# All eight channel blocks of a depthwise convolution on TensorE, in 128x32 column tiles over shifted copies made through DRAM

## The reference

```python
def conformer_conv(x, w_pw1, b_pw1, dw_w, dw_b, ln_g, ln_b, w_pw2, b_pw2):
    a = x @ w_pw1 + b_pw1
    u = a[..., :D_MODEL] * jax.nn.sigmoid(a[..., D_MODEL:])
    u = lax.conv_general_dilated(u, dw_w[:, None, :].astype(u.dtype), window_strides=(1,),
        padding=[(CONV_WIDTH - 1, 0)], dimension_numbers=("NWC", "WIO", "NWC"),
        feature_group_count=D_MODEL) + dw_b
    u = jax.nn.silu(layer_norm(u, ln_g, ln_b))
    return u @ w_pw2 + b_pw2
```

## Time and profile before

| | |
|---|---|
| Time before, median of 3 runs | 1090.81 us (1090.73 to 1091.69) |
| The profiled execution's own time | 1090.82 us |
| Its span in the profile | 1088.8 us |
| PE busy, of the span | 1061.1 us (97%) |
| DVE busy | 706.8 us (65%) |
| ACT busy | 540.7 us (50%) |
| POOL busy | 22.6 us (2%) |

### The profile page before, as it was taken

The page is one execution under the profiler, slowest core; times in us unless marked ns, Lnnn a source line. Parts: engine busy times, 40 slices in busy tenths (PEclk is TensorE's granted clock), DMA queues, the critical chain, the costliest instruction groups (busy, mean ns, idle before and its releaser), DMA issues.

```text
span 1088.8 us, 13626 instructions
## 1 busy us (share of the span) xinstructions
PE 1061.1 (97%) x5484; PEld 899.6 (83%) x5484; DVE 706.8 (65%) x996; ACT 540.7 (50%) x698; POOL 22.6 (2%) x34
## 2 busy tenths in 40 slices
PE   8999899999999999999999999999999999999997
PEld 7998778888887778778888887878888888999886
DVE  5999875544548787776454545767554475777654
ACT  5853654444445666755444434565444553434533
POOL 1000310000000000000000000000000000000000
PEclk9999999999999999999999999999999999999999
DMA  8631365555553453256554555366545455455530
GB/s 322 193 100 39 106 223 197 190 193 193 193 175 144 151 188 117 78 199 246 193 193 174 179 191 191 122 216 232 191 177 194 157 191 193 157 192 193 194 116 39
DMA packets 27829, 188.68 MB, mean 173 GB/s; under 512 B 3016, under 2 KB 4168, under 8 KB 5880
## 3 DMA queue, kind: packets, MB, share of 16 engines
q1 hardware_dynamic: 24912, 179.32, 45.8%
q0 software_dynamic: 1392, 6.21, 1.7%
q10 hardware_dynamic: 1464, 2.30, 1.2%
HBM read 185.19 MB, written 2.62 MB: 173 GB/s over the span
## 4 chain that ended last, share of the span: by engine, by line
PE 88%; DVE 7%; ACT 3%; issue 1%; POOL 0%; ACTq 0%; POOLq 0%; DVEq 0%
PE bank L254 27%; PE bank L256 26%; PE bank L255 26%; PE bank L444 4%; DVE w_lo L1212 3%; PE bank L296 2%; ACT w_hi L764 1%; PE bank L361 1%; PE bank L417 1%; DVE x_lo L1268 1%; DVE arena L1258 1%; ACT x_hi L782 0%; PE bank L502 0%; ACT arena L953 0%; PE bank L458 0%
## 5 line engine op out<-in xcount | busy, mean ns | idle before, releaser
L1212 DVE TENSOR_TENSOR w_lo<-raw,w_hi 128x2048 fp32r<-128x2048 f32 x169 | 389.5, 2309 | 217.3 <-ACT w_hi L764 216.6
L764 ACT ACTIVATE w_hi<-raw 128x2048 fp32r<-128x2048 f32 x169 | 322.4, 1910 | 163.2 <-PE bank L256 156.9
L254 PE MATMUL bank<-w_hi,x_hi 128*128 128x512 f32 x800 | 318.2, 398 | 7.3 <-DVE x_lo L1268 4.8
L256 PE MATMUL bank<-w_hi,x_lo 128*128 128x512 f32 x800 | 313.1, 391 | 0.0
L255 PE MATMUL bank<-w_lo,x_hi 128*128 128x512 f32 x800 | 312.2, 390 | 0.0
L254 PEld LDWEIGHTS bank<-w_hi,x_hi 128*128 128x128 f32 x800 | 150.5, 188 | 42.8 <-issue 6.9
L256 PEld LDWEIGHTS bank<-w_hi,x_lo 128*128 128x128 f32 x800 | 150.6, 188 | 32.4
L255 PEld LDWEIGHTS bank<-w_lo,x_hi 128*128 128x128 f32 x800 | 150.7, 188 | 29.4
L254 PE MATMUL bank<-w_hi,z_hi 128*128 128x512 f32 (+1 forms) x368 | 143.0, 389 | 3.3 <-DVE h L1339 1.5
L256 PE MATMUL bank<-w_hi,z_lo 128*128 128x512 f32 (+1 forms) x368 | 141.7, 385 | 0.0
L255 PE MATMUL bank<-w_lo,z_hi 128*128 128x512 f32 (+1 forms) x368 | 141.6, 385 | 0.0
(11 more groups left out here) (209 smaller groups left out, 791.6 us busy)
## 6 DMA issues: line engine op xcount, KB each, us to landing
raw<-in_ws SPq DMA_DIRECT2D x169, 1024.0 KB, 4.8
arena<-in_rows POOLq DMA_DIRECT2D x2, 1024.0 KB, 5.6
toep<-bias_row ACTq DMA_DIRECT2D x1, 1536.0 KB
h<-in_x_tok SPq DMA_DIRECT2D x2, 512.0 KB, 4.6
arena<-in_rows POOLq DMA_DIRECT2D x2, 512.0 KB, 7.2
arena<-toep POOLq DMA_DIRECT2D x1, 1024.0 KB, 6.8
out<-arena SPq DMA_DIRECT2D x2, 512.0 KB, 2.9
arena<-in_pool_m POOLq DMA_DIRECT2D x1, 768.0 KB, 4.4
```

Source lines behind the costliest of these rows:

```text
L254: pe.matmul(dst, s_hi, m_hi, start=first, stop=False)
L256: return pe.matmul(dst, s_lo, m_hi, start=False, stop=last)
L764: act.activation(w_hi[:, g % SPLIT, :], raw[:, g % RAW, :], ACT.Copy).then_inc(hi_done, 1)
L1212: dve.tensor_tensor(w_lo[:, g % SPLIT, :], raw[:, g % RAW, :], w_hi[:, g % SPLIT, :].bitcast(F32), ALU.subtract).then_inc(lo_done, 1)
```

## The change

All eight blocks go to PE and none to DVE. A float32 matmul of 128x128 that holds a diagonal uses one in 128 of its cells. Instead the 128 rows now hold four shifts of 32 channels, and 32 columns hold these channels: one matmul of a 128x32 column tile does four taps of 32 channels. Four such column tiles (`QUADS`) make up the 128 channels of a block, and eight rounds (`ROUNDS`) make up 32 taps, the last of which is zero. So a block has 32 matmuls of 32x256 outputs.

The moving operand needs each channel on four partitions, shifted by 0, 1, 2 and 3 tokens. ACT makes it through DRAM: `store(f)` writes the block of `u_pad` to `u_scr`, and `spread(f)`, once that has landed, reads it back with four DMAs, one for each shift, into `u_rows` (3 buffers). The stationary tiles are made by POOL, one `tensor_tensor` of 128x1024 for each block (4 buffers), from `lanes` (a 32-column identity on each quarter of the partitions, one DVE reduction) and a new table of 256 columns in `prm`. The copy `toep<-bias_row` and the load of `row_b2` stand behind the eight builds on POOL. The blocks go in the order 0 to 7. `POOL_LO` is empty, so `lo_ready` waits for the same numbers as before.

```diff
-CONV_PE = 5
-PW_ORDER = (0, 5, 1, 2, 6, 3, 4, 7)
+CONV_PE = 0
+PW_ORDER = (0, 1, 2, 3, 4, 5, 6, 7)
+PADDED = 288
+LANE, QUADS, ROUNDS = 32, 4, 8
+SPREAD = 4 * (ROUNDS - 1) + SEQ
...
             def conv_taps(f):
-                i, b = f - CONV_PE, (2, 3, 5)[f - CONV_PE]
-                pe.wait_ge(S("u"), PW_AT[f] + 1)
+                i, b = f - CONV_PE, (5, 2, 3, 6)[f % 4]
+                pe.wait_ge(S("taps_built"), i + 1)
+                pe.wait_ge(S(f"ld_u{i % 3}"), 64 * (i // 3 + 1))
                 begin(b)
-                for q, (t0, nt) in enumerate(TAP_GROUPS):
-                    gr = len(TAP_GROUPS) * i + q
-                    pe.wait_ge(S("diag_built"), gr + 1)
-                    for j in range(nt):
-                        ins = pe.matmul(banks[b][:, 0:SEQ], taps_of[:, gr % DIAGS, j, :], u_pad[:, f, t0 + j:t0 + j + SEQ],
-                                        start=t0 + j == 0, stop=t0 + j == TAPS - 1)
...
+                for q in range(ROUNDS):
+                    for j in range(QUADS):
+                        ins = pe.matmul(banks[b][j * LANE:(j + 1) * LANE, 0:SEQ], taps_of[:, i % 4, q, j, :],
+                                        u_rows[i % 3][:, j, 4 * q:4 * q + SEQ], start=q == 0, stop=q == ROUNDS - 1)
...
+            pw1(0)
+            pw1(1)
+            for f in range(2, KB):
                 pw1(f)
+                conv_taps(f - 2)
+            for f in range(5):
+                mean_of(f, first=f == 0)
             conv_taps(6)
             mean_of(5)
             conv_taps(7)
             mean_of(6)
+            mean_of(7, last=True)
...
+            def build_taps(i):
+                at = PCOL["dw_q"] + ROUNDS * QUADS * i
+                if i >= 4:
+                    s_, v_, _, _ = filled[("conv", i - 4)]
+                    pool.wait_ge(s_, v_)
+                pool.tensor_tensor(taps_of[:, i % 4, :, :, :].rearrange("p q j c -> p (q j) c"),
+                                   lanes.unsqueeze(1).to_broadcast([P, ROUNDS * QUADS, LANE]),
+                                   prm[:, at:at + ROUNDS * QUADS].unsqueeze(2).to_broadcast([P, ROUNDS * QUADS, LANE]),
+                                   ALU.mult).then_inc(S("taps_built"), 1)
+
+            pool.wait_ge(S("ld_par"), 16)
+            pool.wait_ge(S("lanes"), 1)
+            for i in range(KB):
+                build_taps(i)
             pool.dma_start(row_b2, bcast(rows, 0)).then_inc(S("ld_b2"), 16)
+            pool.wait_ge(S("bias_row"), 2)
+            pool.dma_start(toep, bias_row[:, :].unsqueeze(1).to_broadcast([HEADS, P, 384])).then_inc(S("toep_out"), 16)
...
+            def store(f):
+                act.wait_ge(S("u"), PW_AT[f] + 1)
+                act.dma_start(u_scr[f - CONV_PE], u_pad[:, slot[f], :]).then_inc(S("u_out"), 16)
+
+            def spread(f):
+                i = f - CONV_PE
+                act.wait_ge(S("u_out"), 16 * (i + 1))
+                if i >= 3:
+                    take(act, ("conv", f - 3))
+                for t0 in range(4):
+                    act.dma_start(u_rows[i % 3][t0 * LANE:(t0 + 1) * LANE, :, :],
+                                  bass.AP(u_scr.tensor, i * P * PADDED + t0, [[PADDED, LANE], [LANE * PADDED, QUADS], [1, SPREAD]])) \
+                       .then_inc(S(f"ld_u{i % 3}"), 16)
+
+            for f in range(KB):
+                sigmoid(f)
+                if f == 2:
+                    p_split(0)
+                feed(f + 3)
+                store(f)
+                if f >= 2:
+                    conv_out(f - 2)
+                spread(f)
             conv_out(6)
...
-            gated(0)
-            taps_on_vector(0, {2: lambda: feed(3), 6: lambda: gated(5), 9: lambda: feed(4), 12: lambda: gated(1),
-                               14: lambda: p_split(0), 17: lambda: feed(5)})
...
+            for f in range(KB):
+                gated(f)
+                if f == 2:
+                    p_split(0)
+                feed(f + 3)
```

More of the change, by code:

```diff
@@ L59, with build @@
                   ("ffn_g1", 8), ("ple_g0", 8), ("ple_g1", 8), ("attn_g", 8), ("norm_g2", 8), ("c3_w", 24),
-                  ("c3_b", 8), ("q_g", 1), ("k_g", 1), ("sub_g", 1), ("sgu_b", 8), ("dw_w", 8 * TAPS)]:
+                  ("c3_b", 8), ("q_g", 1), ("k_g", 1), ("sub_g", 1), ("sgu_b", 8), ("dw_w", 8 * TAPS), ("dw_q", 8 * 32)]:
     PCOL[_name] = PCOLS
     PCOLS += _n
-CONV_PE = 5
-PW_ORDER = (0, 5, 1, 2, 6, 3, 4, 7)
+CONV_PE = 0
+PW_ORDER = (0, 1, 2, 3, 4, 5, 6, 7)
+POOL_LO = range(0, 0)
 PW_AT = {f: q for q, f in enumerate(PW_ORDER)}
-DIAGS = 4
-PADDED = TAPS - 1 + SEQ
-TAP_GROUPS = [(0, 7), (7, 6), (13, 6), (19, 6), (25, 6)]
-def build(nc, ws, x_tok, p_feat, par, rows, lam_rows, rel, onehot, sgu_w, pool_m, toep, out):
+PADDED = 288
+LANE, QUADS, ROUNDS = 32, 4, 8
+SPREAD = 4 * (ROUNDS - 1) + SEQ
+def build(nc, ws, x_tok, p_feat, par, rows, lam_rows, rel, onehot, sgu_w, pool_m, toep, u_scr, out):
     ctx = ExitStack()
@@ L117, in build @@
         inv_d = view(11760, P)
-        taps_of = view(12032, DIAGS, 7, P)
+        taps_of = view(12032, 4, ROUNDS, QUADS, LANE)
+        lanes = view(11888, LANE)
+        u_rows = [view(6384, QUADS, SPREAD), view(0, QUADS, SPREAD), view(QUADS * SPREAD, QUADS, SPREAD)]
         y_odd = view(9968, 2, SEQ)
-        u_pad = view(2048, KB, PADDED)
+        u_pad = view(2272, 7, PADDED)
+        slot = {f: f % 7 for f in range(KB)}
         y = view(4336, KB, SEQ)
@@ L192, in S, with lo_ready @@
             return ev[name]
+        def lo_ready(eng, g):
+            if g in POOL_LO:
+                eng.wait_ge(S("lo_pool"), g - POOL_LO[0] + 1)
+            else:
+                eng.wait_ge(lo_done, g + 1 - len([p for p in POOL_LO if p < g]))
         def col(name, i=0, n=1):
@@ L460, in mean_of @@
                     end("mean", 0, ins, release=(S("centred"), 4))
-            for f in (0, 5, 1, 2):
+            pw1(0)
+            pw1(1)
+            for f in range(2, KB):
                 pw1(f)
-            conv_taps(5)
-            for f in (6, 3, 4):
-                pw1(f)
+                conv_taps(f - 2)
+            for f in range(5):
+                mean_of(f, first=f == 0)
             conv_taps(6)
-            pw1(7)
-            mean_of(0, first=True)
-            mean_of(1)
-            mean_of(2)
             mean_of(5)
@@ L474, in _ @@
             mean_of(6)
-            mean_of(3)
-            mean_of(7)
-            mean_of(4, last=True)
+            mean_of(7, last=True)
             begin(7)
@@ L703, in _ @@
             pool.memset(inv_d, 1.0 / D).then_inc(S("consts"), 1)
+            pool.memset(u_pad[:, :, TAPS - 1 + SEQ:PADDED], 0.0)
             pool.memset(u_pad[:, :, 0:TAPS - 1], 0.0).then_inc(S("consts"), 1)
@@ L1384, in gated @@
                 dve.wait_ge(S("sig"), q + 1)
-                dve.scalar_tensor_tensor(out=u_pad[:, f, TAPS - 1:], in0=bank[:, 0:SEQ], scalar=col("b_a", f),
+                if f == 7:
+                    dve.wait_ge(S("u_out"), 16)
+                dve.scalar_tensor_tensor(out=u_pad[:, slot[f], TAPS - 1:TAPS - 1 + SEQ], in0=bank[:, 0:SEQ], scalar=col("b_a", f),
                                          in1=sig[:, q % 2, :], op0=ALU.add, op1=ALU.mult).then_inc(S("u"), 1)
-            def taps_on_vector(f, side):
-                last = [0, 0]
-                dve.wait_ge(S("u"), PW_AT[f] + 1)
-                sums = (y[:, f, :], y_odd[:, f % 2, :])
-                for tap in range(TAPS):
-                    if tap in side:
-                        side[tap]()
-                    c, shifted, w = tap % 2, u_pad[:, f, tap:tap + SEQ], col("dw_w", f * TAPS + tap)
-                    if tap == 0:
-                        ins = dve.tensor_scalar(sums[0], shifted, w, col("dw_b", f), ALU.mult, ALU.add)
-                    elif tap == 1:
-                        ins = dve.tensor_scalar(sums[1], shifted, w, None, ALU.mult)
-                    else:
-                        dve.wait_ge(dve_step, last[c])
-                        ins = dve.scalar_tensor_tensor(out=sums[c], in0=shifted, scalar=w, in1=sums[c],
-                                                       op0=ALU.mult, op1=ALU.add)
-                    n[0] += 1
-                    ins.then_inc(dve_step, 1)
-                    last[c] = n[0]
-                dve.wait_ge(dve_step, n[0])
-                dve.tensor_tensor(sums[0], sums[0], sums[1], ALU.add).then_inc(S("conv"), 1)
             bank, free = take(dve, "bias")
@@ L1888 @@
     toep = nc.dram_tensor("toep", (HEADS, P, 384), F32).ap()
+    u_scr = nc.dram_tensor("u_scr", (KB, P, PADDED), F32).ap()
     out = nc.dram_tensor("out_0", (SEQ, D), F32, kind="ExternalOutput").ap()
-    build(nc, *args, toep, out)
+    build(nc, *args, toep, u_scr, out)
     r = run_bass_kernel_spmd(nc, [arrays], core_ids=[0])
```

80 lines of the change are left out of this document (17 added, 63 removed).

## The result

The changed kernel takes 1112.87 us in the median of four runs (1109.2 to 1113.01), the kernel before beside it 1090.77 (1090.71 to 1091.69): 1.0193 of it, 95% interval 1.0171 to 1.0214. It is slower by 1.9% (1.7 to 2.1). The traced execution took 1109.2 us, a span of 1107.2, and what follows explains its 18.4 us over the 1088.8 of before; the other three took 3.6 to 3.8 us more, and no trace shows where.

A forecast was written before the change was run, and what follows sets the result against it. PE was taken to bound the kernel, busy 1061.1 of 1088.8 us. The stretch from the first product on gave -6.3 us, POOL's builds +5.2, the clock +1.0, a memset +0.1: 0.0, so 1090.8 us, range 1084 to 1118.

The forecast's parts named there:

- Elsewhere: Outside taps, DRAM path and start: later builds hidden, DVE's saved splits worth 0, moved toep copy and row_b2 cost 0.
- DRAM's landings: On each block's way from ACT to PE: 2.9 us for a store to land, 4.0 for its spread.
- DRAM sets the pace: Rival (7%), slower: landings of 7.8 us make ACT's round 12.0 against PE's 9.7, some 31 us more, 1122.
- The two waits: PE waits for the way through DRAM: 1.3 us before the first taps and 0.7 before block 7's.
- Taps: On PE, four column tiles side by side: 3.9 us a block (3.5 to 14.2), 31.2 for eight.
- full overlap of four tiles: Forecast for PE's taps: four column tiles work side by side, 3.9 us a block, 1090.8 in all; chance 55%.
- The rivals of program order: PE's taps, slower: tiles start in program order, 7.3 us a block, 1116 (17%); or no overlap, 14.2, 1171 (7%).
- Start: Ahead of the first product: POOL's builds take turns with DVE's splits, PE starts at 22.5 instead of 17.33, +5.2 us.
- Nothing covers it: Of the late start: x_lo released PE at 17.33, so all that follows on PE moves by the 5.2 us.
- Clock: PE has nothing between 16.8 and 22.5; a start from rest was taken as 1.0 us (0 to 2.3).
- the forecast case: Full overlap of the column tiles in PE's taps: 1090.8 us, own range 1085 to 1098, chance 55%.
- the rival of tiles in program order: PE's column tiles start in program order: 7.3 us a block, +27.2 less 2.0 of DRAM waits, 1116; chance 17%.

The follow-up runs named there:

- 3: The kernel before without the copy of bias_row to toep, the bias read from the weights' memory: 1090.2 us, ratio 1.0002.
- 1: The changed kernel with the toep copy issued only once the last block's spread has landed: 1090.86 us, ratio 1.0002 to the kernel before.
- 2: The changed kernel with the toep copy issued by ACT behind the first sigmoid, as before the change: 1116.47 us.
- 9: Against 5, the toep copy issued early again, right behind the last build of taps: 1106.65 us, ratio 1.0135 to the kernel before.
- 12: The changed kernel with only half the rows of the toep copy (768 KB), at the same place: 1098.38 us.
- 4: On top of 1, POOL's builds start only when DVE has split all of x: 1091.3 us, ratio 1.0007 to the kernel before.
- 5: On top of 1, taps one block later and POOL's builds held until the first block is gated: 1080.66 us, ratio 0.9907 to the kernel before.
- 6: Against 5, POOL's builds begin as early as in the changed kernel: 1085.48 us, ratio 0.9958 to the kernel before.
- 11: On top of 1, 36 instead of 10 filling matmuls on PE ahead of the first pointwise block: 1090.68 us, ratio 1.0001 to the kernel before.
- 13: The changed kernel with the toep copy's source exchanged for the parameters' table on 128 partitions, same bytes, place and queue: 1095.33 us.
- 14: The changed kernel with the toep copy's source exchanged for DRAM, same bytes, place and queue: 1097.18 us.
- 8: On top of 1, the taps' two loops exchanged, so all 16 passes of one column tile follow each other: 1154.22 us.

## Why the prediction was wrong, point by point

- **The step that failed** is the last sentence of "Elsewhere": "The `toep` copy and `row_b2` land some 30 us before anyone asks: 0." It priced a moved transfer by its reader alone. The reader did wait for nothing. But the copy of 1.5 MB out of 8 partitions takes 35 us, and the store and the 1 MB piece that were issued behind it took 23.5 and 22.5 us to land. In the old place nothing hung on that (3); in the new order each block's way to PE leads through a store and a spread, and the copy lands among them: 20.05 us, and 2.8 more at half clock behind the pause (1, 2, 9, 12). The trace of before held a sign: the three pieces beside the copy landed in 13.4 to 19.2 us. The prediction took the 7.8 of the earlier trace rows for the pace of this stretch's weights; without the copy that median is 5.1 (3).
- **DRAM's landings.** The rival "DRAM sets the pace" had the right point, a store that takes over 5.5 us, and the wrong cause. It gave up that case because the later stretch has fewer `raw` bytes; the load that mattered was not `raw`. The ordinary store took 3.9 and the spread 5.4 us (taken: 2.9 and 4.0), in 1 the first spread 7.8. The two waits, taken as 2.0 together, were 5.0 in 1 (3.7 and 1.3). The sum also put ACT's split of 1.9 us ahead of the store; the store of block 0 was issued at 32.32, 0.7 us into the split that began at 31.59.
- **Taps: right.** 3.59 us a block against 3.9 (3.5 to 14.2), and full overlap of four tiles (chance 55%). The rivals of program order fell. The switch between widths costs more elsewhere: from one block's taps to the next are 9.54 us, 5.95 for `pw1` beside 5.77 alone, 0.9 us in five blocks.
- **Start: mechanism right, size off.** The first product came 2.9 us late (predicted 5.2). The first build took 1.91 us (2.4 assumed), so `w_lo` was held for 1.0 us and the two first `x_lo` together for 1.7, where the sum had two builds of 2.4 ahead of them. That the scaling of the input would be held too was in the sum (it ended at 11.38, taken: 11.65). "Nothing covers it" was wrong in the order of the change: there an earlier start was lost again in the waits for spreads and in taps at half clock (4). Where no taps waited for the first spread, the builds' turns cost 4.8 us (5, 6).
- **Clock:** 1.0 was taken (0 to 2.3). The records from 22 to 28 come every 0.213 us instead of 0.119, which in 6 us less 0.8 of idling is about 2.3 us. With the copy late it is no price of its own: without it the time is the same (11).
- **The sum for the traced run:** 2.9 us at the start; from there to the centring 107.5 against 91.5: the pause 20.05, the slow clock behind it 2.8, 21.1 for the first three `pw1` (17.3 for three alone), 29.75 for the other five, taps 28.8 besides, means and the last waits 5.0. Without the pause and the slow clock behind it that is 1109.2 - 22.8 = 1086.4, inside the forecast case's own range of 1085 to 1098; with the copy held back the kernel took 1090.86 in the median and 1089.11 in its traced execution, 3.7 of it the wait for the first spread.
- **What agrees by luck.** The measured 1112.87 lies in the range of 1084 to 1118, but the range ran that high for the rival of tiles in program order (1116), which did not occur; a pause behind a copy stood nowhere in it. And that 1 comes out at the forecast 1090.8 is cancelling: up to the centring its traced execution has 2.3 us less than the sum at the start and 2.3 less in the taps, but 3.0 more in waits for spreads and 0.8 more in `pw1` with the clock.

## What to carry to other kernels

Price a moved DMA by what it does to the queues and to the transfers that are issued while it runs, not by its reader; the copy with its source on 8 partitions was slow, and a store issued behind it took up to 33.7 us to land. Where the product of an engine makes a round trip through DRAM, count how many blocks of other work lie between the store and its use: a saving upstream can be lost in that wait until it is covered (4 and 11 gained nothing that could be measured, and later builds gained 4.8 us once the taps stood one block later). Four column tiles gave nearly their full factor (3.59 us against 3.46) with neighbours in the program in different tiles, and little of it (11.43) with one tile behind another.

## What the runs showed of the hardware that was not expected

- **A copy from 8 partitions.** 1536 KB in 35.4 us is 44 GB/s, and 33.9 to 37.0 us in the other kernels; from 128 partitions 14.0, from DRAM 11.2. The Trainium skill, "SBUF — State Buffer", section "Door 1: The DMA port swizzle", says that a transfer's bandwidth depends on how many of 16 ports its partitions reach and puts partitions 0 to 7 on two of them. With the 435 GB/s for all 16 from "DMA: Bandwidth & Descriptors", Specifications, two give 54 GB/s and 29 us, an estimate from these pages. The trace agrees in kind: 35.4 us, and 2.5 times less with a source on all partitions. The pages' ports say nothing of the half of the engines that the copy left idle (12 to 14). No row ahead of the prediction had this copy's duration; the estimate would have come near it.
- **Others behind it.** Stores of 144 KB beside it took 23.5 and 33.7 us where 3.9 is usual, a spread 27.7 instead of 5.4, a 1 MB piece 22.5, and issuing one spread up to 4.5 us where 0.45 is usual. From 100 to 105 us in the changed kernel the DMA share is 0.51, so while the store waited half of the engines' time lay idle. That a store's share on the busy engines waits while the others are done would fit this; no run shows it.
- **Column tiles.** Four float32 tiles in turn: 3.59 us a block. The Trainium skill, "TensorE: Matmul & The Clock Gate", Part 3, The mechanism, has matmuls start and end in program order, by which the second pass of one tile would hold up the next: no less than 32 x 0.216 = 6.9 us a block. The trace disagrees, with 3.59. The first four passes, 0.41 us each in the mean of the page, lie within 0.42 us.

```profile
41.32 0.42 PE L454 MATMUL bank<-arena 128*32 128x256 f32 x4
```

With the tiles one behind another they overlap for about four passes at each seam only (8).
- **Turns between POOL and DVE** also hold an instruction of DVE that reads one large tensor in SBUF, as the prediction had it though the earlier trace rows show only instructions with two: 2.30 us in place of 0.75.
